# A block kernel on one Trainium2 core: the sink logit as a column of the scores, the low parts made elsewhere in the order

## What is computed

```
s_band = jnp.where(valid_band, s_band - slopes * clipdist(dist_band), -jnp.inf)
s_meta = jnp.where(valid_meta, s_meta - slopes * clipdist(dist_meta), -jnp.inf)
sink = jnp.broadcast_to(sinks, s_band.shape[:-1] + (1,))
p = jax.nn.softmax(jnp.concatenate([s_band, s_meta, sink], axis=-1), axis=-1)
o = p_band @ v_band + p_meta @ v_meta          # the sink's share is dropped
return (o * jax.nn.silu(gate)) @ w_out
```

## Time and profile before

| | |
|---|---|
| median of 3 runs | 1648.54 us (1645.93 to 1651.45) |
| the profiled execution's own time | 1648.61 us, its span 1646.8 us |
| PE, DVE, ACT, POOL busy in the span | 97%, 71%, 55%, 6% |
| mean granted TensorE clock | 0.991 |
| sink attention | 1136.8 to 1212.1 us of the span |
| delta projection | 1256.4 to 1433.9 us of the span |

### The profile page before, as it was taken

The page is one execution under the profiler, slowest core; times in us unless marked ns, Lnnn a source line. Parts: engine busy times, 40 slices in busy tenths (PEclk is TensorE's granted clock), DMA queues, the critical chain, the costliest instruction groups (busy, mean ns, idle before and its releaser), DMA issues. The chain is left out here.

```text
span 1646.8 us, 33797 instructions
## 1 busy us (share of the span) xinstructions
PE 1591.8 (97%) x12944; PEld 1427.8 (87%) x12944; DVE 1171.3 (71%) x2011; ACT 905.6 (55%) x1621; POOL 105.3 (6%) x74
## 2 busy tenths in 40 slices
PE   7999999999999999999999999999999998999998
PEld 6888988999999999998888888888768888888877
DVE  5668676789888999986666666657756658655565
ACT  4347753454556767766666666654656544345443
POOL 0000000200000000000000000024002333200000
PEclk9989999999999999999999999999999999999999
DMA  6642355565554444446666666643123444300014
GB/s 221 189 139 80 115 166 156 172 185 165 181 178 152 141 132 139 131 139 206 192 193 195 195 193 191 191 133 106 63 90 103 129 151 145 124 7 3 3 37 144
DMA packets 63077, 229.42 MB, mean 139 GB/s; under 512 B 7008, under 2 KB 7264, under 8 KB 62960
## 3 DMA queue, kind: packets, MB, share of 16 engines
q1 hardware_dynamic: 62960, 227.79, 44.2%
HBM read 226.71 MB, written 1.05 MB: 138 GB/s over the span
## 5 line engine op out<-in xcount | busy, mean ns | idle before, releaser
L1140 DVE TENSOR_TENSOR tile_low<-weights,tile_high 128x1024 fp32r<-128x1024 f32 x252 | 308.1, 1223 | 141.5 <-ACT tile_high L1130 141.3
L1130 ACT ACTIVATE tile_high<-weights 128x1024 fp32r<-128x1024 f32 x252 | 268.1, 1064 | 134.2 <-issue 134.2
L182 ACT ACTIVATE tile_high<-weights 128x1024 fp32r<-128x1024 f32 x168 | 177.3, 1057 | 226.4 <-issue 70.0
L1212 PE MATMUL banks<-parts,tile_high 128*128 128x256 f32 x2048 | 271.9, 286 | 0.9 <-ACT tile_high L1130 0.6
L194 DVE TENSOR_TENSOR tile_low<-weights,tile_high 128x1024 fp32r<-128x1024 f32 x144 | 177.8, 1236 | 128.6 <-ACT tile_high L182 114.3
L1212 PEld LDWEIGHTS banks<-parts,tile_high 128*128 128x128 f32 x2048 | 255.3, 192 | 1.7 <-issue 1.7
L1532 PE MATMUL banks<-tile_high,parts 128*128 128x512 f32 x1024 | 253.0, 389 | 0.9 <-ACT parts L1490 0.9
L1532 PEld LDWEIGHTS banks<-tile_high,parts 128*128 128x128 f32 x1024 | 192.1, 188 | 41.0 <-issue 1.1
L236 PE MATMUL banks<-parts,tile_high 128*128 128x272 f32 (+1 forms) x1184 | 166.9, 294 | 0.2 <-ACT big L316 0.2
L236 PEld LDWEIGHTS banks<-parts,tile_high 128*128 128x128 f32 x1184 | 155.0, 193 | 9.2 <-issue 7.5
L1217 PE MATMUL banks<-parts,tile_low 128*128 128x256 f32 x1024 | 144.4, 284 | 4.1 <-DVE tile_low L1140 4.0
(11 more groups left out here) (411 smaller groups left out, 2202.8 us busy)
## 6 DMA issues: line engine op xcount, KB each, us to landing
weights<-in_peer_u SPq DMA_DIRECT2D x128, 512.0 KB, 3.5
weights<-in_peer_v SPq DMA_DIRECT2D x128, 512.0 KB, 3.5
weights<-in_dn_in SPq DMA_DIRECT2D x49, 512.0 KB, 3.5
weights<-in_in_t SPq DMA_DIRECT2D x19, 512.0 KB, 3.6
weights<-in_attn_t SPq DMA_DIRECT2D x18, 512.0 KB, 3.5
weights<-in_in_m SPq DMA_DIRECT2D x16, 512.0 KB, 3.5
weights<-in_wq SPq DMA_DIRECT2D x16, 512.0 KB, 3.6
weights<-in_dn_out SPq DMA_DIRECT2D x16, 512.0 KB, 3.5
```

The costliest lines, as they stand in the source:

```text
L182: k.nc.scalar.activation(k.high[:, m % 2, :], k.ring.view(n), ACT.Copy).then_inc(*k.high_made.up())
L1130: k.nc.scalar.activation(k.high[:, (s + j) % 2, :], k.ring.buf[:, j % RING, :], ACT.Copy).then_inc(k.high_made.sem, 1)
L1140: k.nc.vector.tensor_tensor(k.low[:, (s + j) % 2, :], k.ring.buf[:, j % RING, :], k.high[:, (s + j) % 2, :].bitcast(F32), ALU.subtract).th ...
L1212: ins = nc.tensor.matmul(ps[:, bank, 0:S], high[:, c, :], x[:, c, :], start=part + c == 0, stop=False)
```

## The change

It has five parts.

1. **The sink is a column.** The keys get a buffer of their own, `keys_padded`, with a column of zeros ahead; the distance table gets the sink logit in its first column. The scores have 145 or 273 columns, and largest score, exp and sum take the sink in with the rest. The three small DVE operations L1763, L1766, L1775 and ACT's L1806 go, 16 times each. Scaling and transposes leave column 0 out.
2. **Low parts one unit on.** DVE makes the low part of a gate tile in unit u+1, behind `scale(u)`.
3. **High parts behind the copies.** ACT makes the high part of the tile ahead at the end of unit u, behind `copy_turned(u-1)`.
4. **Fillers.** PE gets `keep_busy` in three places: 5 calls ahead of `turn(0)`, 3 ahead of the last `turn`, 3 ahead of the last `values`.
5. **The other half of the tiles on POOL.** In the delta projection POOL makes the low parts of the tiles t = 3, 5, ... 47 (23 of them) in place of t = 2, 4, ... 48 (24).

```diff
-        engine = "gpsimd" if k.tiles["dn_in"] + AHEAD <= n < k.tiles["dn_out"] and n % 2 else "vector"
+        engine = "gpsimd" if k.tiles["dn_in"] + AHEAD <= n < k.tiles["dn_out"] and n % 2 == 0 else "vector"
...
-    keys = lambda tt: META + (tt + 1) * P
+    keys = lambda tt: 1 + META + (tt + 1) * P
...
-                                           T[rows, AK + h // 8, 0:keys(tt)], start=True, stop=True)
+                                           k.keys_padded[rows, h // 8, 0:keys(tt)], start=True, stop=True)
...
             def turn(u):
                 tt, _ = units[u]
+                if u == 0:
+                    pe.wait_ge(*copied_v.at(len(spans)))
+                    keep_busy(k, 4, 5)
+                if u == len(units) - 1:
+                    pe.wait_ge(*masked.at(u + 1))
+                    keep_busy(k, 2, 3)
                 pe.wait_ge(*scaled.at(u + 1))
...
             def values(u):
                 tt, a = units[u]
-                pe.wait_ge(*unturned.at(u + 1))
                 if u:
                     pe.wait_ge(*stored.at(u))
+                if u == len(units) - 1:
+                    keep_busy(k, 2, 3)
+                pe.wait_ge(*unturned.at(u + 1))
...
-                nc.vector.tensor_tensor(st[:, s, 0, :], st[:, s, 0, :], sinks[:, 2 * a:2 * a + 2],
-                                        ALU.max).then_inc(*stats.up())
-                dve.wait_ge(*stats.last())
-                nc.vector.tensor_tensor(st[:, s, 3, :], sinks[:, 2 * a:2 * a + 2], st[:, s, 0, :],
-                                        ALU.subtract).then_inc(*stats.up())
...
-                nc.vector.tensor_tensor(st[:, s, 2, :], st[:, s, 2, :], st[:, s, 3, :], ALU.add).then_inc(*stats.up())
...
-                    make_low(dve, k, gate_tile(1))
                 if u:
                     scale(u - 1)
+                if u == 1:
+                    make_low(dve, k, gate_tile(1))
...
-                if u in ahead:
-                    make_low(dve, k, ahead[u])
+                if u - 1 in ahead:
+                    make_low(dve, k, ahead[u - 1])
...
-                nc.scalar.activation(st[:, s, 3, :], st[:, s, 3, :], ACT.Exp).then_inc(*exped.up())
...
-                elif u in ahead:
-                    make_high(act, k, ahead[u])
...
                 if 1 <= u <= len(units):
                     copy_turned(u - 1)
+                if u in ahead:
+                    make_high(act, k, ahead[u])
...
             for tt in range(NT):
                 dist = k.c("dist")[:, L * tt:L * tt + META + (tt + 1) * P]
+                nc.gpsimd.tensor_copy(k.distance[tt][:, :, 0:1], k.p("sinks").unsqueeze(2)).then_inc(*biased.up())
```

More of the change, by code:

```diff
@@ L1620, in refine, with sink_attention_stage @@
     dve.wait_ge(*sig.last())
-def sink_attention_stage(k, meta, taken, keyed, row_chain, biased):
+def sink_attention_stage(k, meta, taken, keyed, row_chain, biased, cleared):
     nc, ps, T = k.nc, k.ps, k.T2
-    AK, GATE = 8, 10
+    GATE = 8
     scored, masked, peaked, exped = k.start("att_scored", "att_masked", "att_peaked", "att_exped")
@@ L1643, in sink_attention_stage @@
     turned_v, copied_v = k.start("values_turned", "values_copied")
-    sinks = k.p("sinks")
     def key_tiles(tt):
-        return [(0, META)] + [(META + i * P, P) for i in range(tt + 1)]
+        return [(1, META)] + [(1 + META + i * P, P) for i in range(tt + 1)]
     stats2, opened = k.start("att_meta_copied", "gate_opened")
@@ L1721, in _ @@
             pe.wait_ge(*keyed.at(4))
+            pe.wait_ge(*cleared.at(2))
             pe.wait_ge(*taken.at(N_ATTN - 1))
@@ L1773, in scale @@
                 s, b, n = u % 2, u % 3, keys(tt)
-                dve.wait_ge(*exped.at(3 * (u + 1)))
-                nc.vector.tensor_tensor(st[:, s, 2, :], st[:, s, 2, :], st[:, s, 3, :], ALU.add).then_inc(*stats.up())
-                dve.wait_ge(*stats.last())
+                dve.wait_ge(*exped.at(2 * (u + 1)))
                 nc.vector.reciprocal(st[:, s, 4, :], st[:, s, 2, :]).then_inc(*stats.up())
@@ L1954, in _ @@
                         for half in range(2):
-                            nc.vector.scalar_tensor_tensor(T[HD * half:HD * half + HD, 8 + g, :], k.keys[mine, :],
+                            nc.vector.scalar_tensor_tensor(k.keys_padded[HD * half:HD * half + HD, g, 1:], k.keys[mine, :],
                                                            k.both_norms[mine, :], r[mine, 2, :], ALU.mult,
@@ L1995, in multiply_scores @@
             ins = nc.tensor.matmul(flat[0:m, place[h % 2]].rearrange("p (h n) -> p h n", n=m)[:, h // 2, :],
-                                   T[rows, h // 2, 0:m], T[rows, AK + h // 8, 0:m], start=True, stop=True)
+                                   T[rows, h // 2, 0:m], k.keys_padded[rows, h // 8, 1:1 + m], start=True, stop=True)
         ins.then_inc(*product.up())
@@ L2055, in second_block @@
     (k.const2, k.T2, k.v2, k.squares2, k.factors, k.soft2, k.pt2, k.y2, k.vT2, k.keys, k.row_factors, k.both_norms,
-     *k.distance) = k.carve(
-        k.big, (n_const,), (18, L), (3, P), (2, L), (4, L), (3, 2, L), (2, 3, 2, P), (KC, L), (L,), (L,), (4, 3 * AH), (1,),
-        *[(AH, META + (tt + 1) * P) for tt in range(NT)])
+     k.keys_padded, *k.distance) = k.carve(
+        k.big, (n_const,), (16, L), (3, P), (2, L), (4, L), (3, 2, L + 1), (2, 3, 2, P), (KC, L), (L,), (L,), (4, 3 * AH), (1,),
+        (2, L + 1), *[(AH, 1 + META + (tt + 1) * P) for tt in range(NT)])
     k.bind("second", k.const2)
@@ L2075, in second_block @@
                  [(k.hm, 0, META, 0)] + [(k.h[:, tt, :], 2 + 2 * tt, P, META + tt * P) for tt in range(NT)],
-                 k.y2, k.tiles["dn_in"] + RING, k.T2[:, 10:18, :], lambda q: opened.at(q + 1), following="dn_in",
+                 k.y2, k.tiles["dn_in"] + RING, k.T2[:, 8:16, :], lambda q: opened.at(q + 1), following="dn_in",
                  scale=[None] + [k.norms[:, 24 + 3 + tt:24 + 4 + tt] for tt in range(NT)],
```

12 lines of the change are left out of this document (5 added, 7 removed).

## The result

| | median, us | runs (lowest to highest) | against before, 95% interval |
|---|---|---|---|
| before, beside it | 1647.53 | 5 (1645.93 to 1651.45) | |
| the changed kernel | 1633.38 | 5 (1632.97 to 1638.93) | 0.9920 [0.9902, 0.9937] |
| the same, second set of runs | 1634.97 | 6 (1633.07 to 1638.49) | 0.9923 [0.9909, 0.9937] |
| the same, third set of runs | 1633.35 | 6 (1632.9 to 1638.98) | 0.9915 [0.9900, 0.9930] |

The change is faster by 0.8%: by the ratio 13.2 us on the median of before beside it, with 10.4 to 16.1 as the interval's ends; the two medians themselves are 14.2 us apart. The profiled execution took 1637.15 us, inside it.

What follows compares the result with a forecast made beforehand. PE carries the kernel, so its waits, its clock and its given work count. Sink stage 3.3 plus delta projection 7.5 makes 10.8 us off 1648.6: 1637.8 us, range 1634.5 to 1642.

Steps and rivals of the forecast that it cites:

- Delta projection: Giving POOL the other half of the tiles' low parts gains 7.5 us: 4.9 + 2.0 + 0.6.
- t = 5: Delta projection, tile iteration 5: PE's 3.65 us wait for the chain and 1.22 us of low clock go, 4.9 us.
- t = 29 to 33: Delta projection: PE's 2.00 us wait at t = 29 goes, a 1.65 wait replaces that of 1.64; net 2.0 us.
- the `finish` waits: Delta projection: iterations with convolution, low part and `finish` cost PE 0.6 us each; three become two, 0.6 us gained.
- new wait: Delta projection: PE waits 1.65 us for DVE's low part of tile 32, in place of the earlier wait of 1.64.
- Rival B: Delta projection, t = 5: the chain meets POOL after all, 4.9 us not gained, 1642.7 us; chance 0.10.
- Reciprocal: Delta projection, t = 29: L1606, one input, does not hold the shared ports; if it did, 0.7 us less gained.
- Sink stage: Waits removed 7.4 + 1.2, clock 1.5, less fillers 7.1, gives 3.0 us; unit by unit 3.6; taken 3.3.
- The waits removed: Sink stage: all 7.4 us of PE's waits for DVE's scaling go, and the 1.2 us ahead of the last values.
- the 1.5 us of clock: Sink stage's start: fillers ahead of `turn(0)` keep PE's clock up, so 1.5 us come back.
- Rival A: Sink stage: the fillers eat its gain, ending within 1 us of before or 1 us behind; 1641.1 us, chance 0.13.
- The range's lower end: Whole kernel: 1635.3 us from the terms' upper bounds 4.2 + 9.1, widened to 1634.5 for the runs' spread.

Runs made afterwards that it cites:

- moves alone: Kernel before with only DVE's low part one unit on and ACT's high part behind the copies, no column or fillers, old parity: 1643.39 us, ratio 0.9972.
- column alone: Kernel before with only the sink as column 0 of scores and distance table, and two PE waits in the changed kernel's order: 1641.93 us, ratio 0.9962.
- sink part alone: Changed kernel with the delta projection's old parity of low parts between POOL and DVE: 1642.29 us, ratio 0.9965.
- no fillers: Changed kernel without its 11 fillers in the sink stage, run twice: 1631.02 us (ratio 0.9895) and 1635.35 us (0.9927).
- values split: Changed kernel without its 11 fillers, the 32 small matmuls of the meta rows' values in two halves in units 5 and 6: 1631.63 us, ratio 0.9905.
- no end fillers: Changed kernel without the two times 3 fillers at the sink stage's last unit, the 5 at its start kept: 1634.64 us, ratio 0.9912.
- meta rows later: Changed kernel without its 11 fillers, DVE's meta-row work spread over later units, run twice: 1629.17 us (ratio 0.9894) and 1633.60 us (0.9912).
- parity alone: Kernel before with one edit, the delta projection's even tiles get low parts from POOL, the odd from DVE: 1639.68 us, ratio 0.9942.

## Why the prediction was nearly right, and where it was not

**Delta projection.** Forecast 7.5, measured 8.4 (176.30 to 167.89 us from the first tile's matmuls to the start of the 49th's low part). The parts: t = 5 gives 5.2 (forecast 4.9), t = 29 to 33 gives 2.2 (2.0), the `finish` waits 1.0 (0.6). The mechanism was the one named at each place, with its new wait of 1.61 us (1.65). What was mis-sized is the price of a wait: the forecast took its recorded length. PE's recorded waits in the stage fall by 6.3 us (10.9 to 4.6) and the low clock at t = 5 by 1.2, which makes exactly 7.5; the other 0.9 lies around the waits. The transposes behind the wait at t = 5 took 0.76 us before and take 0.51, the first `spread` took 0.39 against 0.29 for the next, and a tile with a `finish` wait of 0.6 gives 0.86 from tile to tile (7.50 to 8.36 in the running difference). Rival B, that the chain meets POOL after all, had a margin of 0.4 us against it; the margin came out as 0.46 (chain done at 1274.96, POOL from 1275.42). In the other profiles with the old parity t = 5 costs 5.2 us more than in the changed kernel with one low stretch there (moves alone), and 6.3 and 6.6 with two (column alone, sink part alone): its price varied with the clock, and the single profile held the lower kind. The latter two have a low stretch at t = 29 to 33 as well, and there it costs nothing: with PE slower the wait for the low part of tile 32 is not there, and the three tiles take 13.2 us against 13.6 in before.

**Reciprocal.** The place at which no row could decide is decided: by the Trainium skill (page "SBUF — State Buffer", section "Who interferes with whom") an operation of one input outside the two-port modes doesn't hold the shared ports. The trace agrees: L1606, 1.83 us as with POOL idle, and POOL's low part, 2.40, run side by side from 1357.4.

**Sink stage.** Forecast 3.3, measured 2.2 in the first profile (75.3 to 73.1, scores to output rows) and 3.6 at one low stretch less in the next two. The waits removed are all 8.6 us. The fillers took 7.4 and not 7.1. At the end they cost 2.6 (forecast 2.85, shown by their removal). At the start the 1.5 us of clock were credited to them; the six profiles with column and moves and no fillers at the start have no low clock there, while either edit alone has (1146 and 1142), so the fillers are not needed for it. That DVE being on time keeps the clock up there is argued and not shown: no fillers has a wait of 1.78 us in these units and no fall behind it, the column alone one of 1.75 and a fall. What the fillers did hide was a second wait of 1.78 us, behind the meta rows' subtraction, which the sum lacked. The two errors nearly cancel: 5 fillers cost 0.9 net. Rival A was half right: the fillers ate 3.6 us of the 7.2 that the stage gains without them (119.6, with before's two low stretches, to 112.4 at one).

**The miss.** The terms add to 3.6 + 8.4 = 12.0 us where 10.8 was forecast: 1.2 too little, mostly in t = 5 and `finish`. The step that failed besides is in this sentence of the prediction: "as good as the median of the runs, so I forecast by what the span loses". It puts the change of all stages that the diff leaves alone at nothing. The profiled execution of before had five low stretches in its head (1136.8 us); most executions of the changed kernel are, by time and mean clock, like its third profile, with three (1133.4 us). Of the 15.5 us between these two spans (1646.8 and 1631.3) 3.4 lie in the head, 3.6 in the sink, 8.5 in the tail. 1637.8 - 1.2 - 3.4 gives 1633.2, the group at 1633 in which 11 of 17 executions lie. With the terms alone set right the sum is 1636.6 and lies in the range; by the third profile it is the head that puts the median out of it. The range's lower end followed the terms' bounds and left only 0.8 us for the spread between executions, although the runs of before reach 2.6 us below their median.

**What stays open.** Of 60 executions of before beside the other kernels, 16 (a quarter) are below 1647 us, its lowest group; of the changed kernel 11 of 17 are in its lowest. Before's times don't order by mean clock as the changed kernel's do: the group of 1645.3 to 1646.7 us has 0.991 wherever its clock is recorded, and some of 1647.3 to 1648.4 have 0.992; none of that lowest group was profiled. Why more of the changed kernel's executions have the short head, in code that the change leaves alone, the runs don't tell; with 17 executions chance is not excluded. Which group an execution falls into was not steered by any edit here. The traces do show that the head's length goes with something that is settled in the first 16 us, ahead of every edit: how many of PE's first 32 matmuls run slowly. In before and in the changed kernel's first profile they read
```profile
9.41 5.93 PE L398 MATMUL banks<-rows 128*128 128x128 f32 x32 [9.41 <-DVE rows L384]
```
```profile
9.52 6.75 PE L398 MATMUL banks<-rows 128*128 128x128 f32 x32 [9.52 <-DVE rows L384]
```
with 20 of them slow (0.21 us from start to start) in before and 28 in the other. Over the sixteen profiles 13 or 14 slow ones go with five low stretches in the head, 15 to 18 with three, 20 with four or five, 24 to 27 with six, and 28 with four (three profiles) or six (one). Why it is so is not shown.

## What to carry to other kernels

A low part moved off the engine that serves the critical chain paid 8.4 us by one line, 5.2 of them at one place that was forecast to 0.3: look first for an operation that ends when its neighbour's on another engine does. Fillers are work: put them in only after the engine that is waited for has been put on time, and take them out again to see what they hide; here either of the two ways of relieving DVE did alone, without fillers, at least what both did with them. Price a wait by what goes with it and not by its length alone: 6.3 us of recorded waits and 1.2 of low clock gave 8.4. Where one kernel's executions fall into groups some microseconds apart, place the forecast by stage lengths at a stated number of low-clock stretches, and widen the range by the spread of the stages that nobody touched.

## What the runs showed of the hardware

- The granted clock falls in stretches of 3.4 us or twice that, each 3.4 worth some 1.7 us to a PE that is busy throughout and less, down to nothing, where PE would have waited. In the head their places differ from execution to execution of one kernel: 3 to 6 of them in the same 1133 to 1139 us of untouched code. The Trainium skill (page "TensorE: Matmul & The Clock Gate", section "Part 1: The HAM clock gate (the "warmup" mystery)") says of a kernel's start that the number of slow matmuls varies from run to run; the traces agree. Of the 32 matmuls that PE begins with (L398), 13 to 28 start 0.21 us apart and the rest 0.11. The traces show further that the low clock of the middle of a kernel varies from execution to execution too, for 6 us of 1640, and that the head's part of it goes with how many of those 32 are slow.
- The same wait of 1.28 us was followed by low clock in three profiles (no fillers, twice, and values split) and not in four others (no end fillers; column alone; meta rows later, twice), nor were the like waits of 1.17 to 1.19 us in before, parity alone and moves alone.
- The clock also falls where PE is busy by the records: at the end of 32 matmuls of 16 columns with no idle time, 1.8 to 1.9 us in all, it fell in 13 of 14 profiles, and in neither of the two in which fillers or another unit's work broke them up.
- The reciprocal L1606, one input, kept its time (1.83 us) beside a POOL operation of two (2.40 us). L1613, with two inputs, took 2.66 us beside one and 0.85 at the end of one, where L1615 took 0.43; and one input alone doesn't free an operation: L2227, a scaling by a constant per row, took 2.54 us beside POOL and 0.35 without.
